# Most of the adaLN projection moved into the retention steps, the maxima of w_up into the mLSTM steps

## The reference

```python
mod = jax.nn.silu(c) @ w_ada + b_ada            # 9 rows of c: 1 prompt, 8 samples
sh1, sc1, g1, sh2, sc2, g2 = jnp.split(mod[:, None, :], 6, axis=-1)
h = rms_norm(x, norm1_w) * (1.0 + sc1) + sh1
proj = h @ w_in                                 # 4 head widths for retention, 4 for mLSTM, gates
y_r = head_norm(retention_chunkwise(...)) * silu(rg)
y_m = head_norm(mlstm_chunkwise(...)) * sigmoid(mo)
x = x + g1 * (concat([y_r, y_m]) @ w_out)
h2 = rms_norm(x, norm2_w) * (1.0 + sc2) + sh2
u, val = jnp.split(h2 @ w_up, [D_FF], axis=-1)
u, _ = causal_dwconv(u, fbuf, ffconv_w, ffconv_b)
x = x + g2 * ((jax.nn.silu(u) * val) @ w_down)
```

## Time and profile before

| | us |
|---|---|
| median of 3 runs | 2833.49 |
| lowest and highest | 2827.89 and 2834.66 |
| profiled execution, its own time | 2826.68 |
| its span, first to last instruction | 2824.8 |

### The profile page before, as it was taken

How to read it: one execution, slowest core, us unless ns; L and a number is a source line. 1 busy time by engine, 2 the same in 40 slices (tenths; PEclk the granted TensorE clock), 3 DMA queues, 4 the chain that set the end, 5 groups by cost and what they waited for, 6 DMA issues and landing times. The chain is left out here.

```text
span 2824.8 us, 44984 instructions
## 1 busy us (share of the span) xinstructions
PE 2558.7 (91%) x17400; PEld 1558.7 (55%) x17400; DVE 1638.0 (58%) x3281; ACT 838.1 (30%) x1273; POOL 393.2 (14%) x389
## 2 busy tenths in 40 slices
PE   7798888978898999769959999999999977999998
PEld 1254544546677777635536666666666643444444
DVE  2535555553676776748857777777777755222222
ACT  1233333321454444224432222222222224111110
POOL 0022222220000000002231222221222200000000
PEclk9899999988999999779979999999999988999999
DMA  9714443445011100153312122222122217232321
GB/s 327 218 39 157 139 139 151 180 126 173 24 51 61 56 30 21 35 170 131 128 51 68 52 75 70 75 75 71 56 66 74 71 61 263 79 98 72 104 71 47
DMA packets 194706, 279.32 MB, mean 99 GB/s; under 512 B 16242, under 2 KB 131490, under 8 KB 191796
## 3 DMA queue, kind: packets, MB, share of 16 engines
q1 hardware_dynamic: 192316, 255.12, 28.4%
q10 hardware_dynamic: 2304, 23.07, 2.2%
HBM read 202.95 MB, written 75.21 MB: 98 GB/s over the span
## 5 line engine op out<-in xcount | busy, mean ns | idle before, releaser
L279 PE MATMUL d_po<-d_w,d_a_parts 128*128 128x512 f16 x704 | 268.4, 381 | 28.5 <-DVE d_w L2737 28.5
L280 PE MATMUL d_po<-d_w,d_a_parts 128*128 128x512 f16 x704 | 268.1, 381 | 0.0
L281 PE MATMUL d_po<-d_w,d_a_parts 128*128 128x512 f16 x704 | 268.1, 381 | 0.0
L2261 PE MATMUL py<-h_parts,wide_weights 128*128 128x384 f16 (+1 forms) x792 | 246.2, 311 | 18.0 <-DVE u_p L2397 18.0
L2262 PE MATMUL py<-h_parts,wide_weights 128*128 128x384 f16 (+1 forms) x792 | 246.0, 311 | 0.0
L2263 PE MATMUL py<-h_parts,wide_weights 128*128 128x384 f16 (+1 forms) x792 | 245.9, 310 | 0.0
L279 PE MATMUL prj<-w_heads,h_parts_t 128*128 128x512 f16 x512 | 196.6, 384 | 10.8 <-DVE h_parts_t L873 5.4
L280 PE MATMUL prj<-w_heads,h_parts_t 128*128 128x512 f16 x512 | 196.2, 383 | 0.0
L281 PE MATMUL prj<-w_heads,h_parts_t 128*128 128x512 f16 x512 | 195.9, 383 | 0.0
L279 PE MATMUL m_prj<-m_h,w_heads 128*128 128x128 f16 (+1 forms) x1088 | 179.8, 218 | 11.5 <-DMA m_h<-h_parts 10.2
L2724 DVE SCALAR_TENSOR_TENSOR d_out<-d_po,d_scale,g_p 128x1024 f32<-128x1024 f32 x16 | 20.5, 1284 | 287.4 <-PE d_po L281 287.3
(11 more groups left out here) (432 smaller groups left out, 5672.2 us busy)
## 6 DMA issues: line engine op xcount, KB each, us to landing
wa<-in_w_ada_dram SPq DMA_DIRECT2D x12, 2048.0 KB, 21.2
u_raw<-in_w_up_dram SPq DMA_DIRECT2D x44, 512.0 KB, 5.4
d_a<-act_cols SPq DMA_DIRECT2D x15, 1408.0 KB, 7.1
act_cols<-u_a SPq DMA_DIRECT2D x44, 384.0 KB, 2.4
win_raw<-in_w_in_dram SPq DMA_DIRECT2D x8, 2048.0 KB, 17.1
S_s<-in_w_up_dram ACTq DMA_DIRECT2D x8, 1408.0 KB, 6.0
w_piece<-in_w_up_dram ACTq DMA_DIRECT2D x8, 1408.0 KB, 9.5
u_wd<-in_w_down_dram SPq DMA_DIRECT2D x22, 512.0 KB, 3.8
```

The source lines that it names most:

```text
L279: nc.tensor.matmul(out, left[0], right[0], start=(k == 0), stop=False)
L280: nc.tensor.matmul(out, left[0], right[1], start=False, stop=False)
L281: return nc.tensor.matmul(out, left[1], right[0], start=False, stop=last)
L2261: nc.tensor.matmul(out, left[0], right[0], start=(start and k == 0), stop=False, skip_group_check=True)
```

## The change

Stage one loads and multiplies only the first 4 pieces of `w_ada` (shift and scale of norm 1). The other 8 go one per retention step, steps 2 to 9: SP loads a piece into the half of the `w_in` buffer that is free (`load_late`), PE multiplies it between the scores and projection 3 (`late_part`), DVE adds the bias and the partial sums after `h_lo` (`late_sum`), SP saves the result to DRAM. The product now puts the 8 products of a piece at four different column groups of PE, in turn, so that DVE has four partial sums to add. In stage one, maxima over partitions go through PE (`SpreadMax`) and no longer through POOL; the four additions per piece come between the scale of a `w_in` block and its `cut_lo`, and the loads of the blocks alternate with those of the pieces. Norm 2's factors are computed at the start of mLSTM. The maxima of `w_up` move from the retention steps to mLSTM steps 2 to 12, one piece of 2 MB each. In retention, ACT's queue takes over the stores and loads of the weights that are cut (`next_weights`), and the decode state is loaded at the start.

```diff
+def ada_part(nc, core, bank, weights):
+    for k in range(KC):
+        t = k % 4
+        last = nc.tensor.matmul(bank[NS * t:NS * t + NC9, :], core.cT[:, k, :], weights[:, k, :], start=(k < 4), stop=(k >= 4))
+    return last
...
+    def turn(self, pe, n):
+        pe.wait_ge(self.found, n + 1)
+        pe.transpose(self.bank[0:H, 0:P], self.red[:], self.ident[:]).then_inc(self.turned, 1)
+        pe.wait_ge(self.diag_here, n + 1)
+        pe.matmul(self.bank[:, P:P + H], self.one[:], self.diag[:], start=True, stop=True).then_inc(self.spread, 1)
...
-            for i in range(1, 12):
-                if i >= NB:
-                    sp.wait_ge(wa_used, i - NB + 1)
-                sp.dma_start(wa[:, i % NB], wada[ORDER[i]]).then_inc(wa_in[i % NB], 16)
-                if i in BLOCK_AFTER:
-                    cut.load_block(sp, BLOCK_AFTER.index(i))
+            cut.load_block(sp, 1)
             core.norm1.load_x(sp, io["x_prompt"][0, 0:P], 0, P)
+            for i in range(1, EARLY):
+                sp.dma_start(wa[:, i], wada[i]).then_inc(wa_in[i], 16)
+                cut.load_block(sp, i + 1)
...
-            part(0, 0)
+            part(0)
+            spread.turn(pe, 0)
...
+            for i in range(1, EARLY):
+                spread.turn(pe, i)
+                part(i)
...
+            for b in range(1, EARLY):
+                cut.find_max(dve, b, spread)
+                cut.set_scale(dve, b, spread, steps)
+                add_parts(b)
+                if b < 3:
+                    cut.cut_lo(dve, b)
...
+            def load_late(p, u, first=False):
+                if not first:
+                    sp.wait_ge(s["late_saved"], 16 * p)
+                sp.dma_start(wl, wada[bass.ds(EARLY + p, 1)].rearrange("o p k n -> (o p) k n")).then_inc(s["late_in"], 16)
...
                 project(2, c, T)
                 scores(c - 1, Ta)
+                if p is not None:
+                    late_part(p, c)
                 project(3, c, T)
...
+            def late_sum(p, u, steps):
+                dve.wait_ge(s["late_done"], p + 1)
+                for t in range(4):
+                    ins = nc.vector.tensor_tensor(brow[:, u], late_bank[NS * t:NS * t + NC9, :], brow[:, u], ALU.add)
+                    if t < 3:
+                        steps.then(ins)
+                ins.then_inc(s["late_sum"], 1)
...
                 if Tn:
                     h_lo(c + 1, Tn)
+                if late:
+                    late_sum(*late, steps)
                 state(c - 1)
...
-                if pieces is not None:
-                    find_max(pieces)
...
+            def find_max(j):
+                dve.wait_ge(s["piece_in"], 16 * j + 16)
+                nc.vector.tensor_reduce(core.wmax[:, bass.ds(j, 1)], piece, AX.X, ALU.max, apply_absolute_value=True).then_inc(s["piece_maxed"], 1)
```

More of the change, by code:

```diff
@@ L427, in _, with part @@
             pe.wait_ge(c_here, 1)
[L429 to L436, removed]
-            part(0, 0)
+            def part(i):
+                pe.wait_ge(wa_in[i], 16)
+                ada_part(nc, core, p_mod[:, i, :], wa[:, i]).then_inc(wa_used, 1)
+            part(0)
+            spread.turn(pe, 0)
             pe.wait_ge(small, 16 * 8)
@@ L464, in _ @@
             steps.then(nc.vector.memset(core.norm1.half[:], -0.5))
-            nc.vector.memset(core.w_gate[:], 0.0).then_inc(gates_zero, 1)
+            spread.start(steps)
+            steps.then(nc.vector.memset(core.w_gate[:], 0.0))
             dve.wait_ge(c_tanh, 1)
@@ L481, in factors @@
[L481 to L495, removed]
-                nc.vector.tensor_copy(red[:, 6:8], red[:, 0:2]).then_inc(bound_here, 1)
-                dve.wait_ge(bound_all, 1)
-                power_of_two(nc, steps, red[:, 4:6], red[:, 0:2], core.hinv[:], bits[:])
-                for s in range(2):
-                    for q in range(2):
-                        steps.then(nc.vector.tensor_scalar(core.ab[:, s, q], core.ab[:, s, q], red[:, s:s + 1], None, ALU.mult))
@@ L503, in _ @@
[L503 to L514 removed]
+            add_parts(0)
+            cut.cut_lo(dve, 0)
+            for b in range(1, EARLY):
[4 more added lines that the diff above has]
+                    cut.cut_lo(dve, b)
@@ L515, in _ @@
+            dve.wait_ge(mod_turned, 1)
+            steps.then(nc.vector.tensor_copy(mod[:], col))
+            norm_factors(nc, core, 0, mod, red, steps)
+            nc.vector.tensor_copy(spread.red[:, 0:1], red[:, 2:3]).then_inc(spread.found, 1)
+            scale_factors(nc, core, 0, spread.fold(dve, BOUND, steps), red, bits[:], steps)
             core.norm1.norm(dve, 0, P)
-            cut.find_scale(dve, 3)
-            add_bias(9)
             cut.cut_lo(dve, 3)
-            add_bias(10)
@@ L712, in step @@
                 turn_qk(c - 1, Ta)
+                if not isinstance(before, int) or before:
+                    pe.wait_ge(s["late_sum"], before)
                 if Tn:
@@ L940, in _, with step @@
             gate(0, P)
-            def find_max(j):
-                for u in range(2):
-                    dve.wait_ge(s[f"piece_in{u}"], 16 * j + 16)
-                    nc.vector.tensor_reduce(core.wmax[:, bass.ds(2 * j + u, 1)], piece[u], AX.X, ALU.max, apply_absolute_value=True).then_inc(s["piece_maxed"], 1)
-            def step(c, T, Ta, Tn, Tnn, steps, mask, between=None, pieces=None):
+            def late_sum(p, u, steps):
+                dve.wait_ge(s["late_done"], p + 1)
+                for t in range(4):
+                    ins = nc.vector.tensor_tensor(brow[:, u], late_bank[NS * t:NS * t + NC9, :], brow[:, u], ALU.add)
+                    if t < 3:
+                        steps.then(ins)
+                ins.then_inc(s["late_sum"], 1)
+            def step(c, T, Ta, Tn, Tnn, steps, mask, between=None, late=None):
                 rotate(c, T, steps)
```

319 lines of the change are left out of this document (195 added, 124 removed).

## The result

The changed kernel takes 2842.26 us by the median of six runs (2837.86 to 2842.82), the kernel before 2833.16 by six (2827.89 to 2834.66). The ratio is 1.0032, with a 95% interval from 1.0019 to 1.0044: slower by a third of a per cent, nearly to the microsecond the 2842.4 that was forecast. The trace shows that the single terms did not come out so well: retention missed by 11 us, stage one by 5 in the other direction, and the traces' total is larger than the medians'.

A forecast was written before the change was run, and what follows sets the result against it. It took DMA to bound stage one alone, and work on PE or DVE's chain retention and mLSTM. Terms -30.6 + 13.1 + 26.4 = +8.9 us, on the median 2833.5, gave 2842.4; range 2820 to 2868.

The forecast's parts named there:

- retention: Retention's term: late pieces' products and additions added, maxima of `w_up` and their loads removed; costs 13.1 us.
- stage one: Stage one's term: two thirds of `w_ada` leave, so retention starts at 89.3 instead of 119.91; 30.6 us back.
- steps 11 to 14: Retention steps rid of the maxima of `w_up`: four plain ones take 104.1 us, 6.7 less.
- the price of a maximum: mLSTM steps 2 to 12: 1.1 us each in plain steps, 4.4 with `find_scale` or a cut.
- The product: PE's product of one piece: 9 slots in place of 16, 6.0 us in stage one, 3.9 in retention.
- rival (a): Float32 products overlap four ways: 10.4 us more from stage one, 4 x 2.2 in retention; 2823.2, chance 0.20.
- the ledger: Stage one's chain added up: 22.7 us at first, blocks 1 and 2 19.0 each, end at 89.3.
- The load of x: Odd retention steps 3 to 9: all four taken at 39.3 us, as ACT's queue now carries the weights.
- Rival (d): Retention: the piece lands late, PE waits 6.3 us in each of steps 4, 6 and 8; 2862, chance 0.12.
- The additions: Retention's odd steps: four additions on DVE push `find_scale` by 2.5 us, to 39.3; even steps pay PE's 3.9.

The follow-up runs named there:

- experiment 3: Three kernels altering only the changed kernel's column groups: products paired by group 2843.26 us, all in one group 2877.5, in two groups 2861.97.
- experiment 1: Changed kernel with ACT's 4 MB of weight load and store issued some 10 us earlier in retention steps 4, 6 and 8: 2826.51 us.

## Why the prediction was right, and which of its steps were not

The number held, 2842.4 against 2842.26, and so did the sign and the range. It was the sum of terms of which these held: DMA was no longer the bound of stage one but for one landing; steps 11 to 14 returned to 26.05 us; and mLSTM, where the price of a maximum was taken from the nearest row, a cut in the same place, gave 42.0, 33.9 and 29.35 for 42.4, 33.8 and 29.3, and 28.2 for 26.4 in all.

**The product, mis-sized.** "I take it that the pair stays serial and that the second of one pair overlaps the first of the next" failed. A piece takes 4 slots in place of 9: 3.60 us for 6.0 in stage one, all of it at a granted clock of 0.50, and 1.90 for 3.9 in retention. These are nearly the lower bounds of the forecast, and rival (a)'s mechanism is the true one (experiment 3). Of the 10.4 that (a) named for stage one only 4.6 arrived. The block from 42.21 took 16.8 for the 19.0 of the ledger and the way from the last maximum to retention 25.65 for 28.6. The block before took 17.55, since PE waited 0.67 for its piece to land, and it began 2.0 late: its weights landed at 24.66, 4.9 behind the time at which DVE was free for them and 2.0 behind the ledger's 22.7, a load that the ledger held to be covered.

**The load of x, missed.** "ACT's queue now carries those, so I take 39.3 for all four." The weights no longer queue ahead of the save of y, but they share the DMA engines with the load of x, which the change did not touch. Steps 5, 7 and 9 took 43.1, 44.9 and 42.0; experiment 1 brings them to 37.0 to 37.7. The term was 18 us. The Trainium skill, "DMA: Bandwidth & Descriptors", section Queues, rings and completion order, says that an engine goes round between the queues that have work. The landing of x after 12.4 us agrees in so far as the second queue was here no way past the traffic, only a share in it. Rival (d) had looked at the wrong load: the piece itself was in time, and PE waited 1.6 us in all for the loads of the eight.

**The additions, counted once too often.** The forecast let PE pay 3.9 in the even step and DVE 2.5 in the odd one, with the odd step at 39.3. Step 3, which the load of x left alone, took 36.1: the additions of step 2 already stand ahead of the state that opens step 3, and those of step 3 behind its `find_scale`, so that `find_scale` comes 9.0 behind it as before, and the 2.6 shows in the even step, 30.5 = 26.0 + 1.9 + 2.6. A pair takes 66.6 in place of the forecast 69.2.

So over retention the forecast was too high by some 7 for the product and the additions and too low by 18 for the load of x: 13.1 against 24.1. Stage one's surprise of 4.6 gave back a part. The rest of the agreement is chance. The forecast put +8.9 on the median of the kernel before, whose trace lay 6.8 under it, while the trace of the changed kernel lay at its median: the traces, by which alone the terms can be judged, say +15.7 and +17.6, and the medians +9.1 and +14.3.

## What to carry to other kernels

Work moved out of a stage that DMA bounds is paid for where it lands, and there at the price of the wait that stands behind it: the same four additions a piece cost 3 us at most or 9.8, the same maximum 1.2 or 4.4, by the step that they stood in. When a transfer moves to another queue, list every small load that the next step waits for and ask what is in flight beside it; issuing 4 MB ten us earlier was worth some 16 us. And place filler work in the steps that have the slack, which the length of each step in the timeline tells before anything is run.

## What the runs showed of the hardware

Float32 products of 9 columns overlap across column groups, by their number and not by the order of the program: 16 instructions of 128x512 take 7.04 us in one group, 3.61 in two, 1.90 in four, and 1.92 with the products paired by group. A load of 512 KB that lands in 5.2 us takes 12.4 to 15.1 beside 4 MB on another queue. The product of a piece with four groups takes 3.60 us at a granted clock of 0.50 and 1.90 at 1.00. POOL's stall after an all-reduce moved between 7.08 and 7.73 us for the same work.
